# Windowed and neighbourhood attention taken in steps of two pairs of heads

## What is computed

```python
u = h @ w_in_l                      # q, k, v of mixers A and B, gate_A, gate_B
ya = window_attention(qa, ka, va, ctx_k, ctx_v, sink)     # 8 heads, +-128 tokens
yb = neighbourhood_attention(qb, kb, vb, ctx_k, ctx_v, rpb)   # 8 heads, 8 x 16 window
m = (sigmoid(ga) * (ya @ w_out_a) + sigmoid(gb) * (yb @ w_out_b)) @ w_o
x = x + gate1 * m
x = x + gate2 * swiglu(modulate(rmsnorm(x), shift2, scale2))
```

## Time and profile before

| | |
|---|---|
| median of three runs | 918.42 us (915.38 to 920.15) |
| time of the profiled execution | 915.14 us |
| its span, first to last instruction | 913.3 us |
| TensorE clock granted, mean | 0.998 |
| attention stage in it | from about 165.8 to about 315.1 us |

### The profile page before, as it was taken

How to read it: one execution, slowest core, us unless ns; L and a number is a source line. 1 busy time by engine, 2 the same in 40 slices (tenths; PEclk the granted TensorE clock), 3 DMA queues, 4 the chain that set the end, 5 groups by cost and what they waited for, 6 DMA issues and landing times. The chain is left out here.

```text
span 913.3 us, 16483 instructions
## 1 busy us (share of the span) xinstructions
PE 893.3 (98%) x6235; PEld 836.4 (92%) x6235; DVE 708.4 (78%) x1322; ACT 468.9 (51%) x966; POOL 121.2 (13%) x154
## 2 busy tenths in 40 slices
PE   7999999999999999999999999999999999999997
PEld 5689888778888899999999899999999999999987
DVE  3657898889688779875447868988678888777986
ACT  4763444666676733343236844555445556544543
POOL 0000000000000000000000032322333222333311
PEclk9999999999999999999999999999999999999999
DMA  9854343452345111125304378869998876999766
GB/s 365 348 190 167 139 151 116 150 156 71 128 129 184 57 60 48 52 88 230 115 25 163 115 152 189 191 147 197 206 205 199 184 179 161 208 204 189 174 152 135
DMA packets 51487, 144.26 MB, mean 158 GB/s; under 512 B 5968, under 2 KB 12368, under 8 KB 50128
## 3 DMA queue, kind: packets, MB, share of 16 engines
q1 hardware_dynamic: 31856, 101.33, 33.6%
q0 software_dynamic: 18832, 41.10, 24.0%
q10 hardware_dynamic: 720, 0.77, 0.3%
HBM read 120.64 MB, written 12.19 MB: 145 GB/s over the span
## 5 line engine op out<-in xcount | busy, mean ns | idle before, releaser
L1278 ACT ACTIVATE w_hi<-stage 128x512 fp32r<-128x512 f32 (+1 forms) x186 | 104.6, 607 | 69.4 <-DMA stage<-stage 49.0
L1946 DVE TENSOR_TENSOR w_lo<-stage,w_hi 128x512 fp32r<-128x512 f32 (+1 forms) x186 | 116.9, 668 | 27.8 <-ACT w_hi L1278 27.4
L2522 PE MATMUL ps<-m_hi,w_hi 128*128 128x320 f32 x304 | 93.9, 309 | 0.0
L2522 PE MATMUL ps<-m_lo,w_hi 128*128 128x320 f32 x304 | 93.9, 309 | 0.0
L2522 PE MATMUL ps<-m_hi,w_lo 128*128 128x320 f32 x304 | 93.9, 309 | 0.0
L2522 PE MATMUL ps<-h_hi,w_hi 128*128 128x320 f32 x272 | 84.0, 309 | 0.0
L2522 PE MATMUL ps<-h_lo,w_hi 128*128 128x320 f32 x272 | 84.0, 309 | 0.0
L2522 PE MATMUL ps<-h_hi,w_lo 128*128 128x320 f32 x272 | 84.0, 309 | 0.0
L2522 PE MATMUL ps<-y_hi,w_hi 128*128 128x320 f32 x264 | 81.9, 310 | 1.8 <-DVE w_lo L1946 0.8
L1371 DVE TENSOR_TENSOR w_lo<-stage,w_hi 128x1024 fp32r<-128x1024 f32 x47 | 57.3, 1222 | 33.8 <-ACT w_hi L858 33.4
L858 ACT ACTIVATE w_hi<-stage 128x1024 fp32r<-128x1024 f32 x47 | 49.5, 1061 | 64.2 <-PE ps L2205 36.8
(11 more groups left out here) (278 smaller groups left out, 2384.3 us busy)
## 6 DMA issues: line engine op xcount, KB each, us to landing
stage<-w_main SPq DMA_DIRECT2D x118, 512.0 KB, 4.1
x<-w_ada SPq DMA_DIRECT2D x23, 512.0 KB, 4.5
stage<-stage POOLq DMA_DIRECT2D x38, 256.0 KB, 4.7
qk<-w_ada SPq DMA_DIRECT2D x7, 1024.0 KB, 11.3
scr<-w_main POOLq DMA_DIRECT2D x28, 256.0 KB, 6.0
y_t<-scr POOLq DMA_DIRECT2D x22, 320.0 KB, 6.4
s_second<-w_main POOLq DMA_DIRECT2D x26, 256.0 KB, 6.2
stage<-w_main POOLq DMA_DIRECT2D x19, 256.0 KB, 6.8
```

The costliest lines, as they stand in the source:

```text
L1278: act.activation(w_hi[:, slot, at:at + job_half(j) * P], left_stage(op, j), ACT.Copy).then_inc(left_hi[op], 1)
L1946: dve.tensor_tensor(w_lo[:, slot, w], left_stage(op, j), w_hi[:, slot, w].bitcast(F32), ALU.subtract).then_inc(left_lo[op], 1)
L2522: ins = pe.matmul(ps[:, BANK_OF[op], 0:TH], wt[:, slot, w], right(op, part, j, k), start=k == 0 and n == 0, stop=k == half - 1 and n == 2)
```

## The change

Ten pairs of A are reordered so that a pair of tile `t` and one of tile `t + 1` alternate, and pairs are taken two at a time, in 20 steps (`N_STEPS`). The pairs of a step in mixer A have 128 + 512, 384 + 512, 512 + 128, 512 + 384 and 384 + 384 columns. Scores use four banks (0 to 3) and run two steps ahead; transposes use banks 4 and 5, the outputs of both pairs bank 6, and the gates are made one half of the tokens at a time in bank 7. In place of `s_neg`, `e_sb` and `p_sb` for each head there is one buffer per head, eight in all: the exponentials are written over the scores one column lower, and normalised where they lie. `pt_sb` moves to other tiles and is doubled. The clearing of `vbz` on POOL moves from the start to behind the two copies. The modulation's reductions come two pairs earlier in mixer B. The diff, cut to its core:

```diff
@@ -245
-        nmax, rsum, rinv = (small[:, 20 + 4 * i:24 + 4 * i] for i in range(3))
+        nmax, rsum, rinv = small[:, 20:28], small[:, 28:36], small[:, 36:40]
-        s_neg = [scr[:, i * 520:i * 520 + 513] for i in (0, 1)]
-        e_sb = [scr[:, 1040 + i * 520:1040 + i * 520 + 513] for i in (0, 1)]
-        p_sb = [scr[:, 2080 + i * 512:2080 + (i + 1) * 512] for i in (0, 1)]
-        pt_sb = [scr[:, 3104 + i * 512:3104 + (i + 1) * 512] for i in (0, 1)]
+        s_neg = [scr[:, i * 516 + 1:i * 516 + 514] for i in range(8)]
+        e_sb = [scr[:, i * 516:i * 516 + 513] for i in range(8)]
...
-        PAIRS = [(mixer, t, blk) for mixer in "AB" for t in range(4) for blk in range(5)]
+        PAIRS = [("A", t + j, (blk, (blk + 2) % 5 if blk < 2 else (0, 1, 4)[blk - 2])[j])
+                 for t in (0, 2) for blk in range(5) for j in range(2)]
+        PAIRS += [("B", t, blk) for t in range(4) for blk in range(5)]
...
+        GATE_STEPS, CHUNKS = [], [(g, half, k) for g in range(N_GATE_ATT) for half in range(2) for k in range(KT)]
+        GATE_FIRST, CHUNKS = CHUNKS[:KT], CHUNKS[KT:]
+        for n in (4, 4, 8, 4, 4, 4, 4, 8, 4, 4) + (4, 4, 8, 4, 4, 8, 4, 4, 8, 8):
+            GATE_STEPS.append(CHUNKS[:n])
+            CHUNKS = CHUNKS[n:]
...
@@ POOL
-            nc.gpsimd.memset(vbz[0:64, :, :], 0.0).then_inc(pool_set, 1)
             pool.wait_ge(score_done, 2 * 10)
...
             ins.then_inc(cbc_moved, 1)
+            nc.gpsimd.memset(vbz[0:64, :, :], 0.0).then_inc(pool_set, 1)
@@ ACT
+            exp(0, 0)
+            exp(0, 1)
             split_next(17)
-            exps(1)
-            for p in range(N_PAIRS):
-                copy_pt(p)
-                if p:
-                    take_output(p - 1)
-                if p + 2 < N_PAIRS:
-                    exps(p + 2)
-                if gate_ended(p) is not None:
-                    take_gate(gate_ended(p))
-                g = gate_ended(p - SPLIT_HI_LATER)
+            exp(1, 0)
+            exp(1, 1)
+            take_gate(0, 0)
+            for i in range(N_STEPS):
+                a, b = 2 * i, 2 * i + 1
+                more = i + 1 < N_STEPS
+                copy_pt(a, 0)
+                copy_pt(a, 1)
+                if more:
+                    exp(a + 2, 0)
+                copy_pt(b, 0)
+                copy_pt(b, 1)
+                if more:
+                    exp(a + 2, 1)
+                    exp(b + 2, 0)
+                if half_ended(i):
+                    take_gate(*half_ended(i))
+                if more:
+                    exp(b + 2, 1)
+                take_output(a)
+                take_output(b)
+                g = gate_ended(i - SPLIT_HI_LATER)
                 if g is not None:
                     split_hi(U_GATE + g + RING, (U_GATE + g) % RING)
@@ DVE
                     dve.wait_ge(score_done, r + 1)
+                    if p >= 4:
+                        dve.wait_ge(t_done, r - 7)
...
-                    dve.tensor_scalar(p_sb[hh][:, lo:hi], e_sb[hh][:, lo:hi], rinv[:, q + hh:q + hh + 1], None,
-                                      ALU.mult).then_inc(norm_done, 1)
+                    e = e_sb[r + hh][:, lo:hi]
+                    dve.tensor_scalar(e, e, rinv[:, q + hh:q + hh + 1], None, ALU.mult).then_inc(norm_done, 1)
...
-            for p in range(N_PAIRS):
-                if p + 1 < N_PAIRS:
-                    normalise(p + 1)
-                if p + 2 < N_PAIRS:
-                    negate_scores(p + 2)
-                if ada2_sum(p):
+            for i in range(N_STEPS):
+                a, b = 2 * i, 2 * i + 1
+                more = i + 1 < N_STEPS
+                if more:
+                    negate_scores(a + 2)
+                    negate_scores(b + 2)
+                modulation2(a)
+                if more:
+                    normalise(a + 2)
+                modulation2(b)
+                if more:
+                    normalise(b + 2)
+                g = gate_ended(i - SPLIT_LO_LATER)
...
@@ PE
             def scores(p):
-                if p:
-                    pe.wait_ge(ttr_done, 2 * p)
+                if p >= 2:
+                    pe.wait_ge(ttr_done, 2 * p - 2)
...
             def transposes(p):
-                if p:
-                    pe.wait_ge(pt_done, 2 * p)
                 for hh in range(2):
-                    pe.wait_ge(norm_done, 2 * p + hh + 1)
+                    r = 2 * p + hh
+                    if p:
+                        pe.wait_ge(pt_done, r - 1)
+                    pe.wait_ge(norm_done, r + 1)
...
-            for k in range(GATE_FIRST):
-                gate_step(0, k)
             scores(1)
-            for p in range(N_PAIRS):
-                transposes(p)
-                if p:
-                    outputs(p - 1)
-                if p + 2 < N_PAIRS:
-                    scores(p + 2)
-                for g, k in gate_steps(p):
-                    gate_step(g, k)
-            outputs(N_PAIRS - 1)
-            pe.wait_ge(pt_done, 2 * N_PAIRS)
+            for chunk in GATE_FIRST:
+                gate_chunk(*chunk)
+            scores(2)
+            scores(3)
+            for i in range(N_STEPS):
+                a, b = 2 * i, 2 * i + 1
+                n = len(GATE_STEPS[i]) // 2
+                transposes(a)
+                for chunk in GATE_STEPS[i][:n]:
+                    gate_chunk(*chunk)
+                transposes(b)
+                for chunk in GATE_STEPS[i][n:]:
+                    gate_chunk(*chunk)
+                outputs(a)
+                outputs(b)
+                if i + 2 < N_STEPS:
+                    scores(a + 4)
+                    scores(b + 4)
+            pe.wait_ge(ttr_done, 2 * N_PAIRS)
```

More of the change, by code:

```diff
@@ L551, in ada2_arrived, with half_ended, gate_ended @@
             return 16 * sum(ada2_slot(b) == ada2_slot(a) for b in range(a + 1))
-        def gate_ended(p):
-            return next((g for g, k in gate_steps(p) if k == KT - 1), None) if p >= 0 else None
+        def half_ended(i):
+            return next(((g, half) for g, half, k in GATE_STEPS[i] if k == KT - 1), None) if i >= 0 else None
+        def gate_ended(i):
+            return half_ended(i)[0] if half_ended(i) and half_ended(i)[1] else None
         def grid_cols(tile):
@@ L733, in _ @@
                     load_ada2(ada2_sum(p)[0] + 2)
-                g = gate_ended(p - SPLIT_LO_LATER)
+                g = gate_ended(p // 2 - SPLIT_LO_LATER) if p % 2 else None
                 if g is not None:
                     load_next(U_GATE + g + 2 * RING)
-            late = sum(gate_ended(p) is not None for p in range(N_PAIRS - SPLIT_LO_LATER, N_PAIRS))
+            late = sum(gate_ended(i) is not None for i in range(N_STEPS - SPLIT_LO_LATER, N_STEPS))
             for u in range(U_GATE + N_GATE_ATT - late + 2 * RING, U_WO):
@@ L1032, in take_gate, with exp @@
                     act.wait_ge(ada_dve, N_ADA2)
-                act.activation(halves(gates[g]), slot_ps(3), ACT.Tanh, scale=0.5).then_inc(act_read, 1)
-            def exps(p):
+                act.activation(gates[g][:, half * TH:(half + 1) * TH], ps[:, 7, 0:TH], ACT.Tanh, scale=0.5).then_inc(act_read, 1)
+            def exp(p, hh):
                 mixer, t, blk = PAIRS[p]
@@ L1543, in negate_scores @@
                 lo, hi = columns(*PAIRS[p])
-                if mixer == "A" and blk == 0:
-                    for hh in range(2):
-                        head = t + 4 * hh
-                        dve.tensor_copy(s_neg[hh][:, 512:513], nsink[:, head:head + 1])
                 for hh in range(2):
@@ new lines, in modulation2 @@
+            def modulation2(p):
+                if not ada2_sum(p):
+                    return
+                ada2_part(*ada2_sum(p))
+                if ada2_sum(p) == (ADA2_LATE - 1, 1):
+                    dve.wait_ge(cbc_moved, 1)
+                    dve.wait_ge(ada_dve, ADA2_LATE)
+                    dve.memset(bb[:, :, :, 0:128], 0.0).then_inc(bb_zero, 1)
+                if ada2_sum(p) == (N_ADA2 - 1, 1):
+                    dve.wait_ge(ada_dve, N_ADA2)
+                    for v in range(2):
+                        at = 2 * KT * SCALE2 + v
+                        ins = dve.scalar_tensor_tensor(out=gain[:, 16 + v:32:2], in0=mod[:, at:at + 2 * KT - 1:2],
+                                                       scalar=1.0, in1=vec[:, V_GFFN:V_GFFN + KT], op0=ALU.add,
+                                                       op1=ALU.mult)
+                    ins.then_inc(mod2, 1)
@@ new lines, in _ @@
+            normalise(0)
+            normalise(1)
+            for i in range(N_STEPS):
[11 more added lines that the diff above has]
+                g = gate_ended(i - SPLIT_LO_LATER)
```

150 lines of the change are left out of this document (66 added, 84 removed).

## The result

| | before | after |
|---|---|---|
| median of four runs each, same chip | 916.90 us (913.96 to 920.15) | 904.14 us (900.46 to 907.87) |
| ratio, 95% interval | | 0.9875 [0.9842, 0.9908] |
| profiled execution: time, span | 915.14, 913.3 us | 907.87, 906.1 us |

The change makes the kernel 1.25% faster, 11.5 us by the ratio. The forecast was 11.0 us and 907.4 us. The profiled execution of after is the slowest of its four; what sets it apart lies mostly in its first 40 us and is told at the end. So stages are compared here, not spans.

What follows compares the result with a forecast made beforehand. PE, busy 98% of the span, was taken as the bound, DVE second. Terms -9.9 + 0.3 - 3.4 + 2.0 = -11.0 us took 918.4 to 907.4 us, own range 904 to 910.5, 8 in 10 within 902 to 913.

Steps and rivals of the forecast that it cites:

- order of PE, changes and passages: PE in attention: 58 fewer array-shape changes at 0.17 us, -9.9 us; 20 more transposes-to-gates passages, +0.3 us.
- idle time that goes: PE's idle in attention, mostly waits for DVE at scores and transposes, shrinks with four score banks: -3.4 us.
- new waits from DVE: PE waits for late DVE, mainly mixer A's iterations 3 to 6: +2.0 us, between 0 and 6.
- POOL's hold-up: DVE normalisations slowed beside POOL's copies, now at step 3: counted as nothing, at most 1.5 us.
- Passages: PE going between transposes and gates: 40 become 60, at 0.015 us each, +0.3 us.
- Old waits: PE's waits in the kernel before, such as 1.00 us at scores 2 and 0.85 at transposes: -3.4 us.
- The table of DVE against PE: Iterations 0 to 7: DVE sums to 53.5 us, PE 53.6, level in mixer A; from 3 to 6, 28.2 against 25.7.
- Normalising in place: DVE's multiplication reading and writing the same addresses: still 0.42 us for 384 columns; forecast wrong if over 0.6.
- the one at 916: Rival: passages between kinds of matmul cost, not shape changes, so the gain is 1 to 3 us; chance 0.07.
- The one at 913: Rival: DVE bounds mixer A at 95% or more, ten steps wait 0.6 us each, gain 5 to 6 us; chance 0.15.
- The one without a stall: Rival: DVE's slack suffices, so PE gets no new waits: 905.4 us; chance 0.12.
- The one beyond 922: Rival: DVE's in-place normalisations are slow, about 922 us at 0.8 us each, 951 at 1.15; chance 0.04.

Runs made afterwards that it cites:

- e4: Changed kernel with the attention stage's modulation reductions on DVE over 128 columns instead of 1024: 900.83 us single, stage 132.64 us.
- e5: Kernel before with its attention stage's modulation reductions on DVE over 128 columns instead of 1024: 917.89 us single, stage 147.14 us.
- e8: Changed kernel with POOL's copies and clearing released by DVE's first reduction of pair 10, not pair 9's scores: 904.98 us, ratio 0.9881, stage 135.81 us.
- e9: The changed kernel run again unaltered, for a second profile: 901.98 us, ratio 0.9860, stage 137.30 us.
- e6: Changed kernel with only the clearing of `vbz` on POOL moved back to the start: 904.83 us single, stage 135.22 us.
- e3: Changed kernel with each head's transposes followed by a quarter of the step's gates, 80 more passages, no added shape change: 906.47 us, ratio 0.9869.
- e1: Changed kernel with outputs a, scores a, outputs b, scores b at a step's end, 36 more shape changes: 908.21 us, ratio 0.9885, stage 139.24 us.
- e10: Changed kernel with two `split_lo` on DVE moved from iterations 3 and 6 to iteration 8: 907.91 us, ratio 0.9920, stage 140.93 us.
- e11: Changed kernel with two low parts moved to iteration 8 and POOL's copies released by pair 10's first reduction: 905.78 us, ratio 0.9900, stage 138.99 us.
- e12: Changed kernel with low parts in iteration 8, POOL's copies released by pair 10's first reduction, mixer A's pairs in old order: 905.73 us single, stage 139.09.

## Why the prediction was right

The whole: 11.0 us forecast, 11.5 by the ratio, 12.16 in the stage. The time itself came 3.3 us below 907.4; 1.5 of that is the base, since the kernel before had a median of 916.90 and not 918.42 with its fourth run. By the forecast's own terms, with e4 and e5 as the measure:

| term | forecast | measured | how |
|---|---|---|---|
| order of PE, changes and passages | -9.9 + 0.3 | -12.7 (-12.0 by groups) | PE busy 145.09 - 132.38, both with light DVE |
| idle time that goes | -3.4 | -4.0 | idle 2.05 - 0.26 of e5 and e4, and 2.2 that e5 takes from the kernel before |
| new waits from DVE | +2.0 (0 to 6) | +3.1 | 4.55 that e4 takes from the changed kernel, less the next line |
| POOL's hold-up | 0 (at most 1.5) | +1.4 | e8 |
| sum | -11.0 | -12.2 | |

The measured side rests on single traces of e4 and e5; the stage of one kernel repeats within about 0.1 us (e9), while e6 and e8, which should be alike, differ by 0.6.

- **Order of PE.** The mechanism is the one forecast: shape counts, passages between transposes and gates don't (e3). The price of 0.17 us a change stands too: 0.17 by e1's rows, 0.16 by the rows of after. What the term had wrong is small and adds up to 3 us: a pair of before loses 0.55 and not 0.51 (1.5 us over 40 pairs), since the one pair read had less than most on its transposes and gates; 61 changes went and not 58 (0.5); the passages cost nothing (0.3); and 0.7 of the 12.7 lies at the stage's ends and in waits that e5 counts as busy.
- **Passages.** 0.015 each was forecast from the earlier trace rows, 0 to 0.005 measured (0.4 us for 80).
- **Old waits.** 3.4 against 4.0: near. The wait at the second scores has gone with the four banks.
- **New waits.** Seven stand between 198 and 252 us, five of them in the 190 to 225 us where they were put, in size 0.1 to 0.5 each, ended by normalisations and once by ACT's copy. The table of DVE against PE was right in saying "level". What it missed is that near balance a late DVE costs more than the idle time says, by what PE waits between matmuls that count as busy: 3.1 us, and 2.0 had been taken. Both lie within the 0 to 6 that was given.
- **POOL.** "In iteration 3 they would fall 3.8 us after the start" came out (202.24 - 198.46), and those normalisations took 0.75. The step that failed is the one not written: that POOL, released by the scores of pair 9, starts when DVE is in iteration 3. It started while DVE still had the last normalisations of iteration 2 before it, late by a transfer of 1.2 us that the forecast costed at nothing, and struck these, which began 0.2 us after its first copy. The bound given, 1.5, is about what it cost.
- **Normalising in place** isn't slow: 384 columns take 0.75 for two, as in the earlier trace rows, wherever POOL is silent.

The errors of size, 3 us too little gain on PE and 2.5 us too little loss on DVE and POOL, took each other out. That the sum came within 1.2 us of the stage's 12.2 is in part luck. Of the rivals, the one at 916 is refuted (e3). The one at 913 had its condition met, DVE at 95%, but the loss was 4.5 us and the gain on PE larger. The one without a stall has a number, 905.4, that is nearer to the 904.14 measured than the forecast's, but it is out all the same: PE stood for 2.4 us, and DVE's lateness cost 4.5. The one beyond 922 falls with the 0.75 us of two normalisations in place.

## What to carry to other kernels

Read PE's tiles column as a sequence and count where the shape changes: each change costs 0.14 to 0.18 us here though PE counts as busy, while eighty more passages between groups of one shape cost 0.4 us together. Price a change from the starts within the rows, not from the stage's length or PE's busy time against a kernel that waits. When such a change brings PE level with the next engine, take the load off that engine in both kernels (as e4 and e5 do) before believing the idle column, since part of the gain is paid back there. And before moving an instruction, follow who waits for it on an in-order queue: two low parts moved by some steps held up a load behind them by 5 us, and the stall of PE that followed brought 3.4 us of half the clock with it.

## What the hardware showed that I had not expected

- **The start differs between executions of one program.** The first 40 us of after in the profiled execution:

```profile
0.00:40.00 40.00, 32.70 (x200) 23.35 (x200) 18.32 (x31) 21.58 (x35) 0.56 (x6) 0.83 0.98 386
```

and of e9, the same kernel:

```profile
0.00:40.00 40.00, 32.78 (x234) 24.52 (x234) 20.29 (x35) 23.66 (x39) 0.56 (x6) 1.00 0.97 385
```

PE's granted clock was 0.83 in the one (1.2 GHz for 13.7 us from 18.3 on, after a stretch in which PE was busy for 12.0 of 18.3 us) and 1.00, 2.4 GHz throughout, in the other; the kernel before had 0.96. The stage then begins at 168.79, 163.94 and 165.77 us. All fourteen traces fall in line: the stage begins at 163.9 us with no such stretch, at 165.6 to 166.2 with 3.4 us at 1.2 GHz, at 168.4 with 10.2 and at 168.8 to 169.1 with 13.7. These up to 4.9 us come and go with one and the same kernel, and are more than e6 or e8 changed. Behind the stage, too, 598 to 603 us were taken by the same work. Why the clock falls in one execution and not in another, no run shows.
- **Eighty added passages cost next to nothing** (0.4 us) although they alternate 32-bit transposes with gate matmuls of another type.
- **PE near balance absorbs.** 36 changes of shape, 6.1 us more of PE's work, lengthened e1's stage by 2.05: about 4 us of waiting went, idle or counted as busy, the meeting with POOL among it.
- **A stall costs more than its length.** Behind waits of 3.3 to 3.5 us, e10, e11 and e12 each have 3.4 us at 1.2 GHz. Behind waits of 1.0 us at most, in the other traces, the clock in the stage stayed at 1.00.
